# RWKV core: GpSimd inverts 32x32 diagonal blocks, TensorE keeps one doubling level, chain steps are spread anew

## The chip, the cores and the metric

The kernel runs on one core of a Trainium2 chip. The metric is the device time in microseconds of one execution, as the median of several runs. A core has five engines that run side by side and wait for each other by semaphores: TensorE (PE in the profile), VectorE (DVE), ScalarE (ACT), GpSimd (POOL) and SyncE (SP, which here only issues transfers); 16 DMA engines move the data.

## The reference, cut to what matters

The kernel computes one transformer-like block on 512 latent tokens and 256 context tokens, width 2048: a combined input projection, three mixers side by side (gMLP, RWKV-7, neighbourhood attention), an output projection and an MLP. The change touches only the RWKV-7 mixer, 12 heads of width 64, in two directions:

```python
def step(s, inp):
    r_t, w_t, k_t, v_t, a_t, b_t = inp
    sa = jnp.einsum('dbhvk,dbhk->dbhv', s, a_t)
    s = s * w_t[..., None, :] + sa[..., :, None] * b_t[..., None, :] + v_t[..., :, None] * k_t[..., None, :]
    return s, jnp.einsum('dbhvk,dbhk->dbhv', s, r_t)
```

The scan is computed in chunks of 64 tokens. Within a chunk, the term `sa` couples every token to those before it. So each chunk, head and direction needs the inverse of a 64x64 matrix, identity minus a strictly triangular part, and that inverse is what the changed step computes.

## The kernel before, in words

The program is one stream of stages: modulation vectors, the input projection with attention and gMLP, the RWKV projections (to about 1068 us of the profiled execution), the RWKV core (about 1064 to 1560 us), then output projection and MLP, which keep TensorE busy to the end. The core goes over 6 pairs of heads, j = 0 to 5. The two heads of a pair lie on partitions 0 to 63 and 64 to 127. Along the free dimension lie 24 instances of 64 columns: 12 chunks of 64 tokens in 2 directions.

A "block group" is what `blocks` issues: 16 matmuls of 64x64 (8 instances, 2 heads) into one PSUM bank. One such matmul leaves two records in the trace, so a group shows as 32. For one pair the engines do this, and TensorE has it in this order:

- `lows(j+1)`: the strictly triangular matrices of the next pair, 3 groups and 24 matmuls more (line 821). DVE masks them into LT and LG.
- `inverse(j)`: the 64x64 inverses X and their transposes XT. The 16x16 blocks on their diagonals come ready from GpSimd. Two levels (`LEVELS = [16, 32]`) double the block size: 6 groups "inv", 3 groups "invX" (only the first level must also update X itself) and 6 groups "invT". ACT copies each "inv" result to TT, and DVE places the others under a mask (`copy_predicated`, line 1631). The first group waits for the diagonal blocks (`R["xl"]`).
- z and w (6 groups), `read(j-1)` (line 872) and the mean of pair j-1, `front(j+1)` (7 masked products, 11 turns of operands), tr, nk, rc, `values(j+1)`.
- `chain(j-1, n)`, n = 1 to 10: the sequential pass over the chunks. A step is 4 matmuls (8 records, line 860) for the two directions, then two DVE operations (line 1680); the next step waits for those. Steps 1 to 3 stand beside `lows`, steps 4 to 10 between the groups of `inverse`. `read` needs all ten.

GpSimd's part: SP gathers the diagonal blocks of LG and LT into a DRAM image by 16 transfers (`gather`, lines 522 and 523) and loads the image into Y (line 526), where each of 96 partitions holds two 16x16 blocks. GpSimd does forward substitution in place, for k = 1 to 14 one product and one sum (lines 614 and 615), and turns the result into YT (line 616). SP writes Y and YT to DRAM (4 transfers, lines 532 and 533) and reads them into X and XT by 16 transfers (`scatter`, line 539). Between two pairs GpSimd clears X and XT (lines 619 and 621), since the doubling levels write outside the diagonal.

SP issues in the order written in the code: `gather(j)`, `load_vectors(j+1)`, `scatter(j)`, `load_receptances(j+1)`, `load_late(j)`. `load_vectors(j+1)` (lines 494 to 497, 2.7 MB) waits until `front(j)` has used up the old vectors, and `scatter(j)` is issued behind it. The gather of pair j+1 and its inversion run while TensorE works on pair j. The names in the code's loops are those of the pair being gathered, so in the stretch in which TensorE inverts pair j, SP goes through `gather(j+1)`, `load_vectors(j+2)`, `scatter(j+1)`.

A table `USES` gives every product its PSUM bank and the counts to wait for. It is made by `bank_uses`, which lists the products in TensorE's order.

Of the kernel before, what the change touches and what calls it, by code (L numbers as in the profile page):

```python
# [26 lines left out]
P = 128  # L27
# [26 lines left out]
LEVELS = [16, 32]  # L54
BASE = 16
T = 64
# [36 lines left out]
CHAIN_BESIDE_LOWS = {1: 1, 2: 2, 4: 3}  # L93
# [18 lines left out]
def bank_uses():  # L112
# [28 lines left out]
    for j in range(BPAIRS):  # L141
# [80 lines left out]
def build_block(nc, ada, adarows, stream1, stream2, tokens, xtok, small, bias, lnrows, loraw, out):  # L222
    with ExitStack() as es:
# [4 lines left out]
        lowd, ximg, xtimg = (nc.dram_tensor(n, (8 * NC, 2 * BASE * BASE), F32, kind="Internal").ap()  # L228
# [94 lines left out]
        masks = fc(SMALL_B)  # L323
        pick = lambda n: masks[:, P * n:P * n + P]
        eye = masks[:, P * (2 + 2 * len(LEVELS)):]
        LG, product, Y = fc(NC * T), fc(112), fc(512)
        AH, BH, KH = fc(NI * T), fc(NI * T), fc(NI * T)
        BT, KTT, GT, cV, RH = [fc(NI * T)], [fc(NI * T)], fc(NI * T), fc(TOK), [fc(NL * T)]
        fc(13312 - SMALL_B - NC * T - 112 - 512 - 6 * NI * T - TOK - NL * T)
# [6 lines left out]
        LT = [fc(NI * T)]  # L336
# [7 lines left out]
        fc(10 * SEQ)  # L344
        LT.append(fc(NI * T))
        YT = fc(512)
# [8 lines left out]
        late_h, late_l = ([fm(SEQ, F32R) for _ in range(5)] for _ in range(2))  # L355
# [86 lines left out]
        def subbed(j):  # L442
            return 2 + SUB_STEPS * (j + 1) + 2 * max(0, j - 1)
# [13 lines left out]
        def _(sp):  # L457
# [29 lines left out]
            sp.dma_start(masks, small["b"]).then_inc(R["load"], 16)  # L487
# [24 lines left out]
            def packed(a, d):  # L512
                return a[0:8 * NC, BASE * BASE * d:BASE * BASE * (d + 1)]

            def rows_of(q, a):
                return a[BASE * q:BASE * q + BASE].rearrange("r (c s) -> r c s", s=T)[:, :, BASE * (q % 4):BASE * (q % 4) + BASE]

            def gather(j):
                ready(sp, ("lowT", j, 0), ("lowT", j, 1), ("lowT", j, 2), ("low", j, 0), ("low", j, 1))
                for q in range(8):  # L520
                    to = lowd[NC * q:NC * q + NC].rearrange("c (d r s) -> d r c s", d=2, s=BASE)
                    sp.dma_start(to[0], rows_of(q, LG)).then_inc(R["lg"], 16)
                    sp.dma_start(to[1], both_dirs(LT[j % 2])[BASE * q:BASE * q + BASE, :, 1, BASE * (q % 4):BASE * (q % 4) + BASE]
                                 ).then_inc(R["lg"], 16)
                sp.wait_ge(R["lg"], 256 * (j + 1))
                sp.dma_start(Y[0:8 * NC], lowd).then_inc(R["yl"], 16)

            def scatter(j):
                sp.wait_ge(R["sub"], subbed(j))
                sp.wait_ge(R["xl"], 256 * j)  # L530
                for d in range(2):
                    sp.dma_start(packed(ximg, d), packed(YT if d else Y, d)).then_inc(R["img"], 16)
                    sp.dma_start(packed(xtimg, d), packed(Y if d else YT, d)).then_inc(R["img"], 16)
                sp.wait_ge(R["img"], 64 * (j + 1))
                if j:
                    sp.wait_ge(R["sub"], subbed(j) + 2)
                for q in range(8):
                    for to, image in ((X, ximg), (XT, xtimg)):
                        sp.dma_start(rows_of(q, to), image[NC * q:NC * q + NC].rearrange("c (d r s) -> r (c d) s", d=2, s=BASE)
# [5 lines left out]
            gather(0)  # L545
            load_vectors(1)
# [38 lines left out]
        def _(pool):  # L585
# [20 lines left out]
            a = Y[0:96, :].rearrange("p (h r s) -> p h r s", h=2, r=BASE)  # L606
            at = YT[0:96, :].rearrange("p (h r s) -> p h r s", h=2, r=BASE)
            for j in range(BPAIRS):
                pool.wait_ge(R["yl"], 16 * (j + 1))
                step(G.memset(Y[0:96, :].rearrange("p (h e) -> p h e", h=2)[:, :, 0:BASE * BASE:BASE + 1], 1.0))  # L610
# [1480 lines left out]
```

## Time and profile before

| what | us |
|---|---|
| median of 3 runs (range) | 3180.15 (3172.73 to 3182.63) |
| profiled execution | 3187.81 |
| its span, first to last instruction | 3186.0 |
| PE busy | 2948.1 (93%) |
| DVE busy | 1478.7 (46%) |
| POOL busy | 1135.3 (36%) |
| ACT busy | 686.0 (22%) |

The span is what the trace covers; 1.8 us of the profiled execution lie around it. PE is nearly always busy, but its busy time counts slow and overlapping matmuls as well. So what the change is worth must be read in the core, stretch by stretch.

### The profile page before, as it was taken

The numbers are of one execution on the slowest core, as the hardware profiler recorded it, in microseconds if no ns is written. First come the engines' busy times: TensorE is split into PE (matmuls) and PEld (weight loads), VectorE is DVE, ScalarE is ACT, GpSimd is POOL, SyncE is SP. The second block draws the span as 40 slices with busy tenths as digits, with TensorE's granted clock in tenths as the row PEclk, the third lists the DMA queues.
The fourth block names the chain that finished last, engine by engine and source line by source line (L and its number), as shares of the span: only waits on it lengthen the run. The fifth ranks groups of instructions, "written<-read, shape, count | busy, mean of one in ns | idle before, by whom it ended". The sixth has DMA issues, their size and how long they took to land.

```text
span 3186.0 us, 59462 instructions
## 1 busy us (share of the span) xinstructions
PE 2948.1 (93%) x24772; PEld 2420.3 (76%) x24772; DVE 1478.7 (46%) x1845; ACT 686.0 (22%) x1013; POOL 1135.3 (36%) x674
## 2 busy tenths in 40 slices
PE   5799998899998489999998999999999999999996
PEld 0577886687777489988786888888888888888885
DVE  0676677444866534444425433333333343333336
ACT  0222222102222112122113212122221212122221
POOL 0343343434342112210343444444444444444442
PEclk7799998899999799999999999999999999999998
DMA  9675566532433432223432332332332233233322
GB/s 402 237 242 179 193 216 214 178 79 65 156 104 126 150 80 66 67 71 107 185 94 66 93 99 93 94 99 93 94 98 93 93 98 95 93 96 96 94 93 112
DMA packets 164890, 398.57 MB, mean 125 GB/s; under 512 B 73952, under 2 KB 78048, under 8 KB 157856
## 3 DMA queue, kind: packets, MB, share of 16 engines
q1 hardware_dynamic: 134016, 296.00, 28.9%
q10 hardware_dynamic: 30336, 96.64, 8.7%
q8 instruction: 217, 3.56, 0.5%
q0 software_dynamic: 288, 2.10, 0.2%
q14 instruction: 33, 0.27, 0.0%
HBM read 358.89 MB, written 35.80 MB: 124 GB/s over the span
## 4 chain that ended last, share of the span: by engine, by line
PE 62%; DVE 2%; issue 1%; DMA 0%; ACT 0%; POOL 0%; POOLq 0%; SPq 0%; DVEq 0%; ACTq 0%
PE bank L1062 17%; PE bank L1063 16%; PE bank L1061 16%; PE bank L784 7%; PE bank L800 2%; PE bank L872 1%; PE bank L946 1%; PE bank L944 1%; PE bank L860 1%; DVE buf L1928 0%; DVE buf L1929 0%; PE bank L808 0%; DMA buf<-lnrows 0%; DVE buf L1885 0%; DMA buf<-scaled_keys 0%
## 5 line engine op out<-in xcount | busy, mean ns | idle before, releaser
L627 POOL TENSOR_TENSOR buf<-buf 128x1024 fp32r<-128x1024 f32 x288 | 697.7, 2423 | 1015.9 <-ACT buf L1261 1015.9
L1062 PE MATMUL bank<-buf 128*128 128x512 f32 x2304 | 909.0, 395 | 0.0
L1063 PE MATMUL bank<-buf 128*128 128x512 f32 x2304 | 908.1, 394 | 0.0
L1061 PE MATMUL bank<-buf 128*128 128x512 f32 x2304 | 904.5, 393 | 0.5 <-POOL buf L627 0.4
L1261 ACT CAST buf<-buf 128x1024 fp32r<-128x1024 f32 x288 | 303.4, 1053 | 1262.7 <-PE bank L1063 1261.4
L1061 PEld LDWEIGHTS bank<-buf 128*128 128x128 f32 x2304 | 433.1, 188 | 104.7 <-issue 2.8
L1062 PEld LDWEIGHTS bank<-buf 128*128 128x128 f32 x2304 | 432.4, 188 | 101.6 <-issue 0.5
L1063 PEld LDWEIGHTS bank<-buf 128*128 128x128 f32 x2304 | 432.5, 188 | 96.8
L651 PE MATMUL bank<-buf 128*128 128x512 f32 (+1 forms) x1168 | 431.3, 369 | 20.4 <-POOL buf L594 11.8
L652 PE MATMUL bank<-buf 128*128 128x512 f32 (+1 forms) x1168 | 422.9, 362 | 0.0
L653 PE MATMUL bank<-buf 128*128 128x512 f32 (+1 forms) x1168 | 418.1, 358 | 0.0
L1900 DVE TENSOR_TENSOR buf<-buf 128x512 f32<-128x512 f32 x64 | 156.3, 2442 | 440.0 <-ACT buf L1450 439.5
L592 POOL CAST buf<-buf 128x1024 fp32r<-128x1024 f32 x94 | 112.5, 1197 | 640.7 <-PE bank L653 495.1
L784 PE MATMUL bank<-buf 64*64 64x64 f32 x7488 | 260.4, 225 | 45.2 <-issue 37.1
L784 PEld LDWEIGHTS bank<-buf 64*64 64x64 f32 x7488 | 247.3, 141 | 57.0 <-issue 49.1
L1912 DVE TENSOR_TENSOR buf<-bank,buf 128x512 f32<-128x512 f32 x128 | 88.4, 691 | 413.0 <-PE bank L1063 385.0
L651 PEld LDWEIGHTS bank<-buf 128*128 128x128 f32 x1168 | 225.6, 193 | 67.2 <-issue 21.1
L653 PEld LDWEIGHTS bank<-buf 128*128 128x128 f32 x1168 | 224.8, 192 | 34.7
L652 PEld LDWEIGHTS bank<-buf 128*128 128x128 f32 x1168 | 226.2, 194 | 31.5 <-issue 1.2
L594 POOL TENSOR_TENSOR buf<-buf 128x1024 fp32r<-128x1024 f32 x94 | 243.3, 2589 | 7.5
L1751 DVE SCALAR_TENSOR_TENSOR buf<-buf 128x1024 f32<-128x1024 f32 x120 | 194.3, 1656 | 17.8 <-DMA buf<-adarows 17.6
L1914 DVE TENSOR_TENSOR buf<-buf 128x512 f32<-128x512 f32 x128 | 182.0, 1422 | 17.0
(222 smaller groups left out, 2214.8 us busy)
## 6 DMA issues: line engine op xcount, KB each, us to landing
buf<-stream SPq DMA_DIRECT2D x382, 512.0 KB, 3.6
buf<-adarows ACTq DMA_DIRECT2D x108, 512.0 KB, 4.9
buf<-ada SPq DMA_DIRECT2D x32, 1024.0 KB, 13.1
scaled_keys<-buf ACTq DMA_DIRECT2D x18, 768.0 KB, 5.7
buf<-scaled_keys SPq DMA_DIRECT2D x18, 768.0 KB, 6.7
buf<-adarows SPq DMA_DIRECT2D x20, 512.0 KB, 6.9
buf<-tokens SPq DMA_DIRECT2D x4, 1536.0 KB, 21.2
buf<-bias ACTq DMA_DIRECT2D x6, 1024.0 KB, 6.4
```

The lines of the kernel that those rows point to most:

```text
L594: G.tensor_tensor(wl[n % RING1], raw[n % RINGW], wh[n % RING1].bitcast(F32), ALU.subtract).then_inc(split, 1)
L627: G.tensor_tensor(wl2[b % SPLIT2], raw2[b], wh2[b % SPLIT2].bitcast(F32), ALU.subtract).then_inc(split2, 1)
L651: pe.matmul(dst, wh[slot][:, c:c + P], xh[:, k, cols], start=k == 0, stop=False)
L652: pe.matmul(dst, wh[slot][:, c:c + P], xl[:, k, cols], start=False, stop=False)
L653: mm = pe.matmul(dst, wl[slot][:, c:c + P], xh[:, k, cols], start=False, stop=k == KT - 1)
L784: mm = pe.matmul(bank[hs, T * i:T * i + T], lhs[hs, left(c, d) if left else inst(c, d)], rhs[hs, right(c, d) if right else inst(c, d)], st ...
L1061: pe.matmul(bank[:, :], lh, rh, start=start, stop=False)
L1062: pe.matmul(bank[:, :], lh, rl, start=False, stop=False)
L1063: return pe.matmul(bank[:, :], ll, rh, start=False, stop=stop)
L1261: nc.scalar.copy(wh2[pos % SPLIT2], raw2[pos % RING2]).then_inc(high2, 1)
L1751: ins = V.scalar_tensor_tensor(part, rring[i % RINGR], csil[:, k, 0:1], part, ALU.mult, ALU.add)
L1914: t.step(V.tensor_tensor(xr[:, m, cols], xr[:, m, cols], dtmp[m % 2], ALU.add))
```

## The change

The diagonal blocks become 32x32 (`BASE = 32`), one on each of 96 partitions. GpSimd's substitution goes over k = 1 to 30. TensorE keeps the level that joins two 32x32 blocks into 64x64 (`LEVELS = [32]`): 3 groups "inv" and 3 groups "invT", none of "invX". X is then never written outside its diagonal blocks, and its clearing between pairs goes. Gather and scatter-read need 8 transfers each instead of 16, of twice the bytes per row. Chain steps 1 to 5 stand beside `lows`, 6 to 10 in the shorter `inverse`. Buffers Y, YT, LG, product and the identity `eye` move to other addresses; `eye` gets a load of its own behind the stores of the RWKV projections.

```diff
-LEVELS = [16, 32]
-BASE = 16
+LEVELS = [32]
+BASE = 32
-CHAIN_BESIDE_LOWS = {1: 1, 2: 2, 4: 3}
+CHAIN_BESIDE_LOWS = {0: 1, 1: 2, 2: 3, 3: 4, 4: 5}
...
         for x in range(NX + 1):
             if x < NX:
                 add(("inv", j, x), x % 2, "s")
+            if j and x in (1, 2):
+                chain(j - 1, 5 + 2 * x)
             if x:
...
-            if j:
-                chain(j - 1, 4 + x)
+            if j and x < NX:
+                chain(j - 1, 6 + 2 * x)
...
-                for q in range(8):
-                    to = lowd[NC * q:NC * q + NC].rearrange("c (d r s) -> d r c s", d=2, s=BASE)
+                for q in range(4):
+                    to = lowd[NI * q:NI * q + NI].rearrange("(c d) (r s) -> d r c s", d=2, s=BASE)
                     sp.dma_start(to[0], rows_of(q, LG)).then_inc(R["lg"], 16)
...
                 for d in range(2):
-                    sp.dma_start(packed(ximg, d), packed(YT if d else Y, d)).then_inc(R["img"], 16)
-                    sp.dma_start(packed(xtimg, d), packed(Y if d else YT, d)).then_inc(R["img"], 16)
+                    sp.dma_start(direction(ximg, d), direction(YT if d else Y, d)).then_inc(R["img"], 16)
+                    sp.dma_start(direction(xtimg, d), direction(Y if d else YT, d)).then_inc(R["img"], 16)
                 sp.wait_ge(R["img"], 64 * (j + 1))
                 if j:
-                    sp.wait_ge(R["sub"], subbed(j) + 2)
-                for q in range(8):
+                    sp.wait_ge(R["sub"], subbed(j) + 1)
+                for q in range(4):
...
             gather(0)
+            sp.wait_ge(F["hst"], 64 * BPAIRS)
+            sp.wait_ge(F["ost"], 16 * BPAIRS)
+            sp.dma_start(eye, small["b"][:, SMALL_B - T:]).then_inc(setup, 16)
             load_vectors(1)
...
                 for k in range(1, BASE - 1):
-                    rows, shape = BASE - 1 - k, [96, 2, BASE - 1 - k, k]
-                    part = product[0:96, 0:2 * rows * k].rearrange("p (h r s) -> p h r s", h=2, r=rows)
-                    step(G.tensor_tensor(part, a[:, :, k + 1:, k:k + 1].to_broadcast(shape), a[:, :, k:k + 1, 0:k].to_broadcast(shape), ALU.mult))
-                    step(G.tensor_tensor(a[:, :, k + 1:, 0:k], a[:, :, k + 1:, 0:k], part, ALU.add))
-                step(G.tensor_copy(at.rearrange("p h r s -> p h s r"), a))
+                    rows, shape = BASE - 1 - k, [96, BASE - 1 - k, k]
+                    part = product[0:96, 0:rows * k].rearrange("p (r s) -> p r s", r=rows)
+                    step(G.tensor_tensor(part, a[:, k + 1:, k:k + 1].to_broadcast(shape), a[:, k:k + 1, 0:k].to_broadcast(shape), ALU.mult))
+                    step(G.tensor_tensor(a[:, k + 1:, 0:k], a[:, k + 1:, 0:k], part, ALU.add))
+                step(G.tensor_copy(at.rearrange("p r s -> p s r"), a))
                 if j:
                     ready(pool, ("inv", j - 1, NX - 1))
-                    step(G.memset(X, 0.0))
                     ready(pool, ("z", j - 1, 2), ("w", j - 1, 2))
                     step(G.memset(XT, 0.0))
```

The same moves of the chain stand in TensorE's `inverse` and in VectorE's loop.

On TensorE, the first pair with a chain (j = 1), from its third chain step on. Before (L784 is a block group's matmul, x16 one group; L860 a chain step's; L821 the rest of `lows`):

```order
L784 MATMUL bank<-buf 64x64 x16
L860 MATMUL bank<-buf 64x64 x4
L784 MATMUL bank<-buf 64x64 x48
L860 MATMUL bank<-buf 64x64 x4
L784 MATMUL bank<-buf 64x64 x48
L860 MATMUL bank<-buf 64x64 x4
L784 MATMUL bank<-buf 64x64 x48
L860 MATMUL bank<-buf 64x64 x4
L784 MATMUL bank<-buf 64x64 x32
```

Now, the whole stretch from the fourth chain step to the last (L788, L864 and L825 are the same lines as L784, L860 and L821 before):

```order
L825 MATMUL bank<-buf 64x64 x16
L864 MATMUL bank<-buf 64x64 x4
L825 MATMUL bank<-buf 64x64 x8
L864 MATMUL bank<-buf 64x64 x4
L788 MATMUL bank<-buf 64x64 x16
L864 MATMUL bank<-buf 64x64 x4
L788 MATMUL bank<-buf 64x64 x16
L864 MATMUL bank<-buf 64x64 x4
L788 MATMUL bank<-buf 64x64 x16
L864 MATMUL bank<-buf 64x64 x4
```

Between two chain steps there stood up to three groups in the inverse; now there is one, and every part of `lows` has a step behind it.

On SP, the scatter of a pair and the transfers ahead of it. Before (L494 begins the loads of the next pair's vectors, L532 writes the DRAM image, L539 reads it):

```order
L494 DMA buf<-scaled_keys 128x1536
L495 DMA buf<-scaled_keys 128x1536
L496 DMA buf<-scaled_keys 128x1536
L497 DMA buf<-values_bonus_gates 128x768
L532 DMA inverse_blocks<-buf 96x256
L533 DMA turned_inverse_blocks<-buf 96x256
L532 DMA inverse_blocks<-buf 96x256
L533 DMA turned_inverse_blocks<-buf 96x256
L539 DMA buf<-inverse_blocks 16x24x16
```

Now:

```order
L496 DMA buf<-scaled_keys 128x1536
L497 DMA buf<-scaled_keys 128x1536
L498 DMA buf<-scaled_keys 128x1536
L499 DMA buf<-values_bonus_gates 128x768
L534 DMA inverse_blocks<-buf 48x1024
L535 DMA turned_inverse_blocks<-buf 48x1024
L534 DMA inverse_blocks<-buf 48x1024
L535 DMA turned_inverse_blocks<-buf 48x1024
L541 DMA buf<-inverse_blocks 32x24x32
```

The order is the same; the image's rows are 4 KB instead of 1 KB, and the reads are 8 of 32x24x32 instead of 16 of 16x24x16.

## Rows read from the trace of the kernel before

**Rows 1.** Stretches: us; busy PE, PEld, DVE, ACT, POOL; granted clock, DMA share, GB/s

```profile
1119.68:1181.81 62.13, 57.26 (x1848) 56.44 (x1849) 23.34 (x38) 13.19 (x23) 13.44 (x32) 0.97 0.30 76
1181.81:1255.88 74.07, 66.77 (x2101) 64.50 (x2101) 33.28 (x60) 16.28 (x27) 13.42 (x32) 0.98 0.27 71
1255.88:1328.64 72.76, 67.04 (x2101) 64.54 (x2101) 33.34 (x60) 15.00 (x26) 13.40 (x32) 0.97 0.28 73
1328.64:1401.04 72.40, 68.22 (x2101) 65.92 (x2101) 33.34 (x60) 15.00 (x26) 13.41 (x32) 0.96 0.28 72
1401.04:1466.40 65.36, 62.41 (x1957) 60.31 (x1958) 30.02 (x53) 14.99 (x26) 13.40 (x32) 0.97 0.22 46
```

**Rows 2.** Timeline of PE (start, duration): two groups in a row; inverse(3)'s first group

```profile
1290.69 1.10 PE L800 MATMUL bank<-buf 64*64 64x64 f32 x32
1291.62 1.10 PE L784 MATMUL bank<-buf 64*64 64x64 f32 x32
...
1325.47 0.43 PE L860 MATMUL bank<-buf 64*64 64x64 f32 x7
1328.64 1.97 PE L784 MATMUL bank<-buf 64*64 64x64 f32 x32 [2.74 <-issue]
```

**Rows 3.** Timeline of SP's issues: first gather and scatter; scatter(3), then gather(4)

```profile
1075.65 0.32 SPq L522 DMA_DIRECT2D diagonal_blocks<-buf  x1
...
1090.89 0.32 SPq L526 DMA_DIRECT2D buf<-diagonal_blocks  x1
...
1109.53 0.32 SPq L539 DMA_DIRECT2D buf<-inverse_blocks  x1
...
1306.25 0.34 SPq L494 DMA_DIRECT2D buf<-scaled_keys  x1
...
1308.91 0.37 SPq L532 DMA_DIRECT2D inverse_blocks<-buf  x1
...
1317.40 0.32 SPq L539 DMA_DIRECT2D buf<-inverse_blocks  x1
...
1325.74 1.29 SPq L539 DMA_DIRECT2D buf<-turned_inverse_blocks  x1
...
1328.19 0.32 SPq L522 DMA_DIRECT2D diagonal_blocks<-buf  x1
...
1336.00 0.45 SPq L523 DMA_DIRECT2D diagonal_blocks<-buf  x1
```

**Rows 4.** Timeline of POOL: first and last instruction of an inversion; inversion(4) starts

```profile
1093.37 0.15 POOL L610 MEMSET buf<- 96x32 f32 x1 [66.96 <-DMA buf<-diagonal_blocks]
...
1105.21 1.06 POOL L616 COPY buf<-buf 96x512 f32<-96x512 f32 x1
...
1342.22 0.15 POOL L610 MEMSET buf<- 96x32 f32 x1 [51.90 <-DMA buf<-diagonal_blocks]
```

**Rows 5.** Groups on POOL by form, 1090 to 1432 us (busy us, mean ns)

```profile
L616 POOL COPY buf<-buf 96x512 f32<-96x512 f32 x6 | 6.3, 1055 | 0.4
...
L615 POOL TENSOR_TENSOR buf<-buf 96x112 f32<-96x112 f32 x12 | 4.9, 407 | 0.9
...
L614 POOL TENSOR_TENSOR buf<-buf 96x28 f32<-96x28 f32 x12 | 2.8, 237 | 1.1 <-POOL buf L610 0.2
```

**Rows 6.** Timeline of DVE: in front(3), the output of pair 1; two later operations

```profile
1302.89 0.68 DVE L1640 TENSOR_TENSOR buf<-buf 128x512 f32<-128x512 f32 x1
...
1306.11 0.69 DVE L1645 TENSOR_TENSOR buf<-buf 128x512 fp32r<-128x512 f32 x1
...
1554.74 3.35 DVE L1637 RECIPROCAL buf<-buf 128x512 f32<-128x512 f32 x1 [6.38 <-ACT buf L1293]
...
2017.98 1.93 DVE L1914 TENSOR_TENSOR buf<-buf 128x512 f32<-128x512 f32 x1
```

**Rows 7.** Timeline of POOL beside the last two rows of the group above

```profile
1555.82 2.40 POOL L627 TENSOR_TENSOR buf<-buf 128x1024 fp32r<-128x1024 f32 x1 [5.34 <-ACT buf L1261]
...
2016.96 2.40 POOL L627 TENSOR_TENSOR buf<-buf 128x1024 fp32r<-128x1024 f32 x1 [3.15 <-ACT buf L1261]
```

More of the change, by code:

```diff
@@ L322, in build_block @@
         fc = lambda n, dt=F32: take(n, dt, core)
-        masks = fc(SMALL_B)
+        masks = fc(SMALL_B - T)
         pick = lambda n: masks[:, P * n:P * n + P]
-        eye = masks[:, P * (2 + 2 * len(LEVELS)):]
-        LG, product, Y = fc(NC * T), fc(112), fc(512)
+        LT = [None, fc(NI * T)]
         AH, BH, KH = fc(NI * T), fc(NI * T), fc(NI * T)
         BT, KTT, GT, cV, RH = [fc(NI * T)], [fc(NI * T)], fc(NI * T), fc(TOK), [fc(NL * T)]
-        fc(13312 - SMALL_B - NC * T - 112 - 512 - 6 * NI * T - TOK - NL * T)
+        fc(13312 - SMALL_B + T - 7 * NI * T - TOK - NL * T)
         VT, late, RB, RK = [fc(TOK)], [fc(2 * SEQ)], [fc(NL * T)], [fc(NL * T)]
@@ L335, in build_block @@
         AT, GV, TT, XT, X = (fc(NI * T) for _ in range(5))
-        LT = [fc(NI * T)]
+        LT[0] = fc(NI * T)
         VT.append(fc(TOK))
@@ L343, in build_block @@
         TR = fc(NI * T)
-        fc(10 * SEQ)
-        LT.append(fc(NI * T))
-        YT = fc(512)
+        fc(8 * SEQ)
+        Y, YT, LG, product, eye = fc(1024), fc(1024), fc(NC * T), fc(240), fc(T)
         core.close()
@@ L354, in build_block @@
         over_tr = [fm(SEQ, F32R) for _ in range(NI * T // SEQ)]
-        late_h, late_l = ([fm(SEQ, F32R) for _ in range(5)] for _ in range(2))
+        late_h, late_l = ([fm(SEQ, F32R) for _ in range(4)] for _ in range(2))
+        late_h.append(fm(SEQ, F32R))
+        late_l.append(fm(SEQ, F32R))
         mix.close()
@@ L442, in subbed @@
         def subbed(j):
-            return 2 + SUB_STEPS * (j + 1) + 2 * max(0, j - 1)
+            return 2 + SUB_STEPS * (j + 1) + max(0, j - 1)
         block = es.enter_context(nc.Block())
@@ L486, in _ @@
             sp.wait_ge(used1, N1)
-            sp.dma_start(masks, small["b"]).then_inc(R["load"], 16)
+            sp.dma_start(masks, small["b"][:, 0:SMALL_B - T]).then_inc(R["load"], 16)
             def load_vectors(j):
@@ L892, in inverse @@
                         if x == 0:
-                            pe.wait_ge(R["xl"], 256 * (j + 1))
+                            pe.wait_ge(R["xl"], 128 * (j + 1))
                         blocks(("inv", j, x), LT[j % 2], X, g)
+                    if j and x in (1, 2):
+                        chain(j - 1, 5 + 2 * x)
                     if x:
@@ L902, in inverse @@
                         blocks(("invT", j, y), TT, XT, gy)
-                    if j:
-                        chain(j - 1, 4 + x)
+                    if j and x < NX:
+                        chain(j - 1, 6 + 2 * x)
             pe.wait_ge(z_ev, TILES[-1][-1][2])
@@ L1663, in lows @@
                 if n == 0:
-                    dve.wait_ge(R["lg"], 256 * j)
+                    dve.wait_ge(R["lg"], 128 * j)
                 if n < 3:
@@ L1700, in dve_core @@
                 for x in range(NX + 1):
+                    if j and x in (1, 2):
+                        chain(j - 1, 5 + 2 * x)
                     if x:
@@ L1706, in dve_core @@
                         placed(("invT", j, y), XT, 3 + 2 * l, g)
-                    if j:
-                        chain(j - 1, 4 + x)
+                    if j and x < NX:
+                        chain(j - 1, 6 + 2 * x)
                 for g in range(3):
@@ L1718, in dve_core @@
                     key = ("tr", j, g)
+                    if j == 0 and g == 0:
+                        dve.wait_ge(setup, 80)
                     V.tensor_tensor(wide8(TR, g), eight(use(dve, key)), eye[:, None, :].to_broadcast([P, 8, T]), ALU.add
```

22 lines of the change are left out of this document (11 added, 11 removed).

## The prediction

> **What bounds the kernel now.** I read the stretches of the core first, one from the first group of inverse(j) to that of inverse(j+1) [rows 1]; I call these starts I0 to I5, so I0 is 1119.68 and I5 is 1466.40. Three full stretches take 74.07, 72.76 and 72.40 us, and in them PE is busy for 67 to 68 us. DVE (33 us) and POOL (13.4 us) have room. So PE is near the bound, but not alone: in front of I3 it idles 2.74 us [rows 2]. The view calls this "issue", yet SP's timeline names the releaser: the last read of the diagonal blocks is issued at 1325.74 and takes 1.29 us [rows 3], and PE starts at 1328.64, when it has landed. The idle time costs again afterwards: the first group behind it takes 1.97 us where a group at full clock takes 1.10 us [rows 2], since the clock had fallen in the idle time to the lower of its two levels (1.2 instead of 2.4 GHz; group times 1.97 and 1.10).
>
> Then I followed the loop of GpSimd backwards from I3 [rows 3]. The scatter's first write is issued at 1308.91, right behind load_vectors (1306.25), which waited for front(3). POOL had begun inversion 3 long before. An inversion lasts from 1093.37 to 1105.21 + 1.06 = 1106.27, 12.9 us [rows 4]. The one for pair 4 starts at 1342.22, 13.6 us behind I3, and would be over at I3 + 26.5, while the scatter in the stretch before went out 53.0 us behind its I2 = 1255.88. So a ready result waits some 26 us for its turn on SP. This is the cover in which a longer inversion may hide.
>
> **The change, part by part.**
>
> *TensorE, removed.* A pair loses 3 groups inv, 3 invX and 3 invT, 9 of 32 records. Two groups in a row start 1291.62 - 1290.69 = 0.93 us apart [rows 2], so 9 x 0.93 = 8.4 us a pair, 50 us over six. That is the most that can be won, apart from idle time that goes too.
>
> *GpSimd, added.* Before, 28 operations work on 2,240 elements per partition. Now 60 operations work on 2 x (30 x 1 + 29 x 2 + ... + 1 x 30) = 9,920. From 237 ns at 28 elements (a product) and 407 ns at 112 (a sum) [rows 5] the slope is 2.0 ns an element at most; with 10 ns of it put down to the sum, 1.9, and 0.19 us are left at zero elements. The whole before, 12.9 us, less the copy (1.06) and the clearing of the diagonal (about 0.25), is 11.6 us for 28 operations, which leaves 0.07 to 0.08 us between two. So: 60 x (0.19 + 0.08) = 16.2, 9,920 x 1.93 ns = 19.1, copy 2 x 1.06 = 2.1, clearing 0.25: 37.7 us. From below, 36.5 (slope 1.8). From above, the nearest long operation is 2.40 us for 1,024 elements [rows 7], 2.16 ns each, which makes 40. I take 37.8.
>
> *GpSimd and DVE together.* The inversion now reaches into the time in which DVE makes the output of the pair before: four products or sums of two SBUF operands, 0.69 us each, between 1302.89 and 1306.80 [rows 6]. Such an operation excludes one of POOL's: at 2017.98 one took 1.93 us and ended 0.55 us behind POOL's operation, which began at 2016.96 and took 2.40 [rows 6, 7]; 0.69 is its plain length. The reciprocal (3.35 us) excludes nothing: POOL's 2.40 us went by beside it at 1555.82. So POOL loses about 4 x 0.69 plus the cast, 3.2 us, in the stretches 1 to 4; between 0 and 7 (if the reciprocal counts). DVE loses at most one short operation of POOL's each time, some 2 us, within its idle 40 us.
>
> The Trainium skill, "SBUF — State Buffer", section "SBUF: two separate sides", says that the port pair shared by VectorE and GpSimd is an exclusive lock, held for a whole instruction. By that rule, the trace agrees in the product and not for the reciprocal; held to the letter for the reciprocal too, it would make the loss 6.5 us in each of four stretches and the sum 13 us worse; without any lock the sum would be 13 us better.
>
> *Transfers.* The gather loses 8 of its 16 issues. 16 take from 1328.19 to 1336.45, 0.5 us each [rows 3], so POOL starts 13.6 - 3.9 = 9.7 us behind I. The total of packets is the same, of 128 B instead of 64 B; if packets and not issues set the pace, nothing is saved (13.6). The scatter's writes take 3.3 us when nothing is ahead of them (1106.27 to 1109.53) and 8.5 behind load_vectors (1308.91 to 1317.40) [rows 3, 4]. The reads take 1328.64 - 1317.40 = 11.2 us for 16, so 11.2 - 8 x 0.5 = 7.3 for 8; 11.2 at worst, 6 at best.
>
> *Not costed.* The memset of X (1.4 us) goes from behind the inversion, where it hid. The load of `eye` waits for stores issued at about 1075 and stands ahead of load_vectors(1), which waits until 1095 anyway. Chain steps 1 to 5 beside `lows` wait for each other somewhat more (a step with its DVE half took 0.8 us where nothing stood between), but they run ahead of I, where PE idles for the diagonal blocks; steps 6 to 10 may cost 1 us. The moved buffers cost nothing.
>
> *The sum.* New loop of GpSimd: 9.7 + 37.8 + 3.2 + 3.3 + 7.3 = 61.3 us. The loads go out at about I + 42 (front is 8.4 us earlier than 50.4) and are nearly over when the writes start at I + 50.7. TensorE's own loop: 72.76 - 2.74 - 8.4 = 61.6, and 74.07 less the same is 62.9. The two are level: I take 62.
>
> - I0: POOL starts some 5 us earlier (8 issues less in front of 1090.89), then 37.8 - 12.9 = 24.9 longer, then reads 3 shorter: +17 us. PE has nothing to do here, so all of this is paid.
> - I0 to I1: 9.7 + 37.8 + 3.3 + 7.3 = 58.1 against 62.1: -4.0.
> - I1 to I2, I2 to I3, I3 to I4: 62 against 74.1, 72.8, 72.4: -12.1, -10.8, -10.4.
> - I4 to I5: 61.4 against 65.4, in which PE did not wait: -4.0.
> - Behind I5: -8.4, +2.5 for the lower clock after a wait that wasn't there, +1 for the chain: -5.
>
> Together -29 us. Everything behind the core is PE-bound and only moves forward. The profiled execution, 3187.8, would become 3159; it lies 7.7 us above the median of the runs, so the median becomes 3180.15 - 29 = 3151 us.
>
> **The rivals.**
>
> 1. *GpSimd stays in the cover.* The inversion is 36.5 us, nothing excludes, reads take 6. Then its loop is 56 us and PE sets the pace at about 59.5, since without idling it keeps its clock. I0 +14, then -6, three times -13 and I4 to I5 -7, tail -7: -45 us, 3135. For it speaks that the inversion before took the same 12.9 us beside a busy and beside an idle DVE; against it, that it needs every term at its favourable end.
>
> 2. *The gain is eaten.* Transfers of the same number of packets save nothing (gather 13.6, reads 11.2), or exclusion costs 7 us. The first adds 7.8 us to each of five loops and to I0, and PE's loop, level with GpSimd's, hides none of it: -29 + 6 x 7.8 = +18 at its full size, at half of it -6, so 3174 us, which I take for it. The even pace of 0.5 us per issue at 192 as at 384 packets speaks against the full size; the occasional issue of 1.2 us and more [rows 3] speaks for some.
>
> 3. *Slower: the long inversion.* If an element costs over 2.6 ns, since rows are now 32 elements apart and the patterns are longer, the inversion is above 44 us. The loop is then 68 us and I0 +24; each further us counts six times. It breaks even at 37.8 + 29 / 6 = 42.6 us and is slower by 0.3% from about 44.2 us. At 46 us it is 20 us slower, 3200. For it speaks only the 2.16 ns of the long operation, against it that the operation at k = 1 (28 rows of one element) and at k = 14 (2 rows of 14) cost the same 230 to 250 ns.
>
> The Trainium skill, "GPSIMD Engine Reference", section "Performance pitfalls for Q7 kernels", gives about 2.9 instead of 1.9 cycles for an element read at a stride above 8 bytes. As an estimate from that page, 9,920 elements would then take 24 us, the inversion 43 us, and the change would end near zero. The product already reads one column at a stride of 64 B in this trace, at 1.9 ns an element, so this rule adds nothing that the rows don't hold; it is part of rival 3.
>
> **How the numbers follow.** The forecast has 0.58, with a range of its own from -42 to -13 us (3138 to 3167): each us of inversion counts six times. Rival 1 has 0.17, rival 2 0.15, rival 3 0.06; 0.04 are for a start of the core that is delayed otherwise. A difference below 0.3%, 9.5 us, is about what a measurement of this kernel can't tell from none. Faster: forecast and rival 1 and a third of rival 2 with a little less, 0.82; same 0.11; slower 0.07. The range leaves out the lowest and the highest tenth: 3131 to 3180.
>
> **What would show it.** POOL's inversion: 60 operations in 35 to 36 us, 37.8 with the copy; 41 in the stretches 1 to 4, where a single operation of POOL's takes 0.7 us longer. I0 at about 1137; the stretches at 58, 62, 62, 62, 61. PE's records fall by 1,728. PE idles for the reads in front of every I, and its first groups behind run at the lower clock. SP issues the scatter behind POOL's copy, not behind load_vectors. Wrong would be: stretches above 66, an inversion above 42 us, or stretches below 60 in which PE never waits (rival 1).

## The result, and the profile after

| | kernel before | changed kernel |
|---|---|---|
| median (lowest to highest) | 3181.39 us (3172.73 to 3185.61) | 3147.80 us (3139.02 to 3149.67) |
| profiled execution | 3187.81 | 3147.17 |
| its span | 3186.0 | 3145.1 |

The ratio is 0.9895 (95% interval 0.9876 to 0.9915): 33 us faster, where 29 were forecast. A later comparison (experiment 11) gave 0.9886 (0.9871 to 0.9902).

I take the profiled executions apart at these marks: the first block group of the core (C), I0, I5, the start of the last reciprocal on VectorE (R) and the end. "Core" is C to R.

| | to C | C to I0 | I0 to I5 | I5 to R | core | R to end |
|---|---|---|---|---|---|---|
| before | 1064.3 | 55.4 | 346.7 | 88.4 | 490.4 | 1631.3 |
| changed | 1056.6 | 73.3 | 308.9 | 79.8 | 462.0 | 1626.6 |
| difference | -7.8 | +17.9 | -37.8 | -8.6 | -28.5 | -4.7 |

The part ahead of C has the same code in both; in the other profiles of this study C lies anywhere from 1051.6 to 1062.6, so the 7.8 us are no effect of the change. The core gives 28.5 us, and 4.7 come from a place that the forecast had left at zero, the hardware loop of the MLP.

The stretches of the changed kernel, to be held against [rows 1] (columns as there):

```profile
1129.83:1188.52 58.69, 48.94 (x1576) 48.28 (x1577) 19.75 (x36) 11.41 (x20) 33.45 (x63) 0.94 0.39 103
1188.52:1251.56 63.04, 60.25 (x1812) 57.71 (x1814) 29.85 (x52) 14.49 (x24) 34.83 (x63) 0.95 0.39 107
1251.56:1314.73 63.17, 57.40 (x1817) 54.84 (x1815) 30.90 (x57) 13.21 (x23) 34.82 (x63) 1.00 0.35 91
1314.73:1377.19 62.46, 57.63 (x1812) 54.95 (x1813) 29.98 (x53) 13.22 (x23) 34.84 (x63) 1.00 0.39 109
1377.19:1438.74 61.55, 54.02 (x1669) 51.11 (x1669) 28.12 (x51) 13.21 (x23) 34.92 (x63) 0.98 0.24 54
```

58.7, 63.0, 63.2, 62.5 and 61.6 us, forecast 58.1, 62, 62, 62 and 61.4. PE has some 288 records fewer in a stretch (1,728 in all, as forecast), POOL is busy for 33 to 35 instead of 13.4 us.

PE's timeline in front of I0, I1, I2, I3 and I5, to be held against [rows 2]:

```profile
1129.83 3.38 PE L788 MATMUL bank<-buf 64*64 64x64 f32 x60 [28.64 <-issue]
...
1188.52 1.98 PE L788 MATMUL bank<-buf 64*64 64x64 f32 x32 [8.22 <-issue]
...
1251.23 0.52 PE L864 MATMUL bank<-buf 64*64 64x64 f32 x8 [0.37 <-DVE buf L1686]
1251.56 1.14 PE L788 MATMUL bank<-buf 64*64 64x64 f32 x32
...
1314.73 1.15 PE L788 MATMUL bank<-buf 64*64 64x64 f32 x32 [1.42 <-issue]
...
1438.74 1.97 PE L788 MATMUL bank<-buf 64*64 64x64 f32 x32 [4.32 <-issue]
```

PE waits 28.6, 8.2, 0, 1.4 and 4.3 us for the diagonal blocks. In I0, I1 and I5 GpSimd's loop decides, at I2 (and I4, whose group has no idle time either) TensorE, at I3 both arrive nearly together. The first group takes 1.15 us behind a wait of 1.4 us, at a granted clock of 1.00, and 1.97 behind one of 4.3, at 0.50: in this profile only the longer idle times brought the clock down to 1.2 GHz.

SP's timeline of scatter(2), to be held against [rows 3] (L496 load_vectors, L534 the first write, L541 the first and the last read):

```profile
1229.60 0.34 SPq L496 DMA_DIRECT2D buf<-scaled_keys  x1
...
1237.11 0.49 SPq L534 DMA_DIRECT2D inverse_blocks<-buf  x1
...
1242.12 0.32 SPq L541 DMA_DIRECT2D buf<-inverse_blocks  x1
...
1246.31 1.50 SPq L541 DMA_DIRECT2D buf<-turned_inverse_blocks  x1
```

The loads go out 7.5 us ahead of the first write, which now waits for POOL alone. POOL's timeline: the start of inversion(0), its sum of 198 elements and its last instruction, then of inversion(3) the start, three operations beside VectorE's output, and the end, to be held against [rows 4]:

```profile
1081.22 0.15 POOL L615 MEMSET buf<- 96x32 f32 x1 [62.00 <-DMA buf<-diagonal_blocks]
...
1107.77 0.57 POOL L620 TENSOR_TENSOR buf<-buf 96x198 f32<-96x198 f32 x1
...
1115.96 1.91 POOL L621 COPY buf<-buf 96x1024 f32<-96x1024 f32 x1
...
1263.80 0.15 POOL L615 MEMSET buf<- 96x32 f32 x1 [25.27 <-DMA buf<-diagonal_blocks]
...
1289.10 0.92 POOL L620 TENSOR_TENSOR buf<-buf 96x210 f32<-96x210 f32 x1
1290.10 0.60 POOL L619 TENSOR_TENSOR buf<-buf 96x198 f32<-96x198 f32 x1
1290.77 0.91 POOL L620 TENSOR_TENSOR buf<-buf 96x198 f32<-96x198 f32 x1
...
1300.06 1.94 POOL L621 COPY buf<-buf 96x1024 f32<-96x1024 f32 x1
```

The same time on DVE's timeline, to be held against [rows 6]:

```profile
1284.16 3.34 DVE L1643 RECIPROCAL buf<-buf 128x512 f32<-128x512 f32 x1
...
1288.74 0.83 DVE L1646 TENSOR_TENSOR buf<-buf 128x512 f32<-128x512 f32 x1
...
1290.34 0.90 DVE L1648 TENSOR_TENSOR buf<-buf 128x512 f32<-128x512 f32 x1
1291.27 0.95 DVE L1649 TENSOR_TENSOR buf<-buf 128x512 f32<-128x512 f32 x1
```

Inversion(0), beside which VectorE runs only operations that read one operand from PSUM, lasts from 1081.22 to 1117.87, 36.65 us; the one for pair 3 from 1263.80 to 1302.00, 38.2 us. The difference, 1.5 us, lies where VectorE makes its output. A sum of 0.6 us takes 0.9 there, and VectorE's operation 0.83 to 0.95 instead of 0.68 to 0.69 [rows 6].

The rows say by how much. POOL's sum starts at 1290.77, when VectorE's operation (1290.34, 0.90 us) has 0.47 us to go, and takes 0.34 us more than in inversion(0). VectorE's next one starts at 1291.27, when that sum has 0.41 us to go, and takes 0.26 more. VectorE's one at 1290.34 found POOL's product (1290.10, 0.60 us) with 0.36 to go and took 0.21 more. So each operation is longer by what is left of the other's, less 0.13 to 0.15 us. The pair in [rows 6, 7] fits too: at 2017.98 POOL's operation had 1.38 us to go, and VectorE's took 1.24 more than its 0.69. The rows fit two engines that take turns, an instruction each. Neither lost the other's whole length, since each time the other was under way already.

POOL's groups by form, 1070 to 1500 us, to be held against [rows 5]:

```profile
L621 POOL COPY buf<-buf 96x1024 f32<-96x1024 f32 x6 | 11.7, 1950 | 0.4
...
L620 POOL TENSOR_TENSOR buf<-buf 96x240 f32<-96x240 f32 x12 | 8.0, 670 | 0.9
```

A sum of 240 elements takes 670 ns; the 0.19 us and 1.93 ns an element of the prediction make 0.65.

### The profile page after: what moved, and what is told of

Read it like the earlier page. It is cut to its first block, busy times and chain, and to the rows that moved or that the text cites. A ratio compares the mean times of both kernels' runs of the same rounds, so it can differ in the third digit from the quotient of the medians.

```text
span 3145.1 us, 56010 instructions
## 1 busy us (share of the span) xinstructions
PE 2894.3 (92%) x23044; PEld 2368.9 (75%) x23044; DVE 1453.2 (46%) x1809; ACT 674.2 (21%) x995; POOL 1269.2 (40%) x861
## 4 chain that ended last, share of the span: by engine, by line
PE 61%; issue 2%; DVE 2%; DMA 0%; ACT 0%; POOL 0%; SPq 0%; DVEq 0%; ACTq 0%; POOLq 0%
PE bank L1068 17%; PE bank L1069 17%; PE bank L1067 17%; PE bank L788 6%; PE bank L804 2%; PE bank L876 1%; PE bank L864 1%; PE bank L952 1%; PE bank L950 1%; DVE buf L1938 0%; DVE buf L1939 0%; PE bank L812 0%; DMA buf<-scaled_keys 0%; DVE buf L1895 0%; PE bank L825 0%
## 5 line engine op out<-in xcount | busy, mean ns | idle before, releaser
L1922 DVE TENSOR_TENSOR buf<-bank,buf 128x512 f32<-128x512 f32 x128 | 88.4, 691 | 413.1 <-PE bank L1069 385.1
L788 PE MATMUL bank<-buf 64*64 64x64 f32 x5760 | 203.6, 224 | 59.6 <-issue 52.7
L788 PEld LDWEIGHTS bank<-buf 64*64 64x64 f32 x5760 | 191.2, 140 | 71.2 <-issue 61.5
L1761 DVE SCALAR_TENSOR_TENSOR buf<-buf 128x1024 f32<-128x1024 f32 x120 | 187.2, 1597 | 20.4 <-DMA buf<-adarows 20.1
```

The costliest lines, as they stand in the source:

```text
L788: mm = pe.matmul(bank[hs, T * i:T * i + T], lhs[hs, left(c, d) if left else inst(c, d)], rhs[hs, right(c, d) if right else inst(c, d)], st ...
L1761: ins = V.scalar_tensor_tensor(part, rring[i % RINGR], csil[:, k, 0:1], part, ALU.mult, ALU.add)
```

## The experiments

**1. Is a result of GpSimd's really lying ready for 26 us in the kernel before?** The kernel before, with the inversion made longer by harmless work:

```diff
+                for _ in range(50):
+                    step(G.tensor_tensor(product[0:96, 0:112], Y[0:96, 0:112], Y[0:96, 0:112], ALU.mult))
```

> The kernel before with GpSimd's inversion lengthened alone, by 50 operations of 96x112 behind the substitution (0.48 us apart, so 24 us, to about 37 us). Nothing on TensorE changes. Theory (the scatter's place behind load_vectors on SP covers a longer inversion): I0 +24; I0 to I1 +4 (the inversion ends 10 us after the old turn, but the writes then have no loads ahead of them); the full stretches and I4 to I5 +0 to +1. Together +28 us, 3209 us. Rival (every added us is paid in each of six inversions): +144 us. Rival (the cover is smaller than 26 us, since the loads collide): +40 to +60 us.

Measured: 3205.78 us, ratio 1.0057 (1.0036 to 1.0077), some 18 us slower, less than the 28 expected; in the profiled execution, the longest of the four (3213.61), the core is 29.5 us longer (519.9), of which 20.8 lie ahead of I0. The inversion grew by 22.3 us (12.9 to 35.2). Without cover it would have cost six times that. SP's timeline of a scatter in this kernel (L495 begins the loads, L533 is the first write), POOL's copy having ended at 1326.71:

```profile
1327.71 0.34 SPq L495 DMA_DIRECT2D buf<-scaled_keys  x1
...
1331.24 0.36 SPq L533 DMA_DIRECT2D inverse_blocks<-buf  x1
```

The result is ready 1.0 us before the loads of the vectors go out and 4.5 us before its own write: the cover is there, and it is now nearly used up. I0, which has none, pays nearly in full.

**2. What bounds the changed kernel once GpSimd is fast?** The changed kernel with k up to 14 only; it leaves out a part of the inverse.

```diff
-SUB_STEPS = 2 + 2 * (BASE - 2)
+SUB_STEPS = 2 + 2 * 14
-                for k in range(1, BASE - 1):
+                for k in range(1, 15):
```

> The changed kernel with the substitution stopped at k = 14 of 30, which leaves out 32 operations and 5,440 of 9,920 elements (the inverse is then incomplete): the inversion takes about 19 us less. Theory (GpSimd's loop and TensorE's are level, TensorE has no slack behind it): I0 -19; I0 to I1 -10; the four later stretches -1 to -6 each as the waits and the lower clock behind them go. Together -35 to -42 us against the changed kernel, about 3108 us. Rival (GpSimd's loop alone sets the pace, TensorE is far from its bound): near -100 us. Rival (TensorE alone sets it): -19 us, the first inversion only.

Measured: 3125.85 us, ratio 0.9809 (0.9783 to 0.9835), 27 us less than the changed kernel's ratio gives, for 35 to 42 expected. The inversion is 18.2 us, half of it, and yet the full stretches stay:

```profile
1163.30:1228.96 65.66, 60.08 (x1819) 57.62 (x1817) 29.62 (x55) 14.48 (x24) 17.33 (x31) 0.95 0.36 98
1228.96:1291.58 62.62, 57.46 (x1816) 54.88 (x1814) 29.74 (x57) 13.20 (x23) 17.29 (x31) 1.00 0.36 97
1291.58:1357.01 65.43, 58.88 (x1813) 56.19 (x1813) 28.98 (x54) 13.20 (x23) 17.27 (x31) 0.97 0.37 103
```

In the profile the core is 19.7 us shorter (442.3): 18.4 less from C to I0 and 8 less in the stretches I0 to I1 and I4 to I5, but 5 more in the three full stretches and 1.7 more behind I5. So TensorE's own loop is 62.6 to 65.7 us here, and not the 59.5 of rival 1. In it stand pauses for which the trace has no releaser, in the middle of a row of matmuls whose data are long there:

```profile
1274.52 0.28 PE L950 MATMUL bank<-buf 64*64 64x64 f32 x4
1278.12 0.27 PE L952 MATMUL bank<-buf 64*64 64x64 f32 x3 [3.32 <-issue]
```

Less such pauses of over 0.7 us (4.5, 3.3 and 5.3 us in the three) the stretches are 61.2, 59.3 and 60.1 us, near rival 1's 59.5. The row of the queue that brings instructions, for 1275.0 to 1276.8 us of this kernel (packets, MB, share):

```profile
q8 instruction: 1, 0.02, 3.4%
```

This packet, a fetch of 16.4 KB, landed at 1276.80, 1.3 us before PE went on. It is no single case. In the 14 kept profiles, from I0 to R, there are 162 such pauses, the waits in front of I0 to I5 left out. 146 of them end 1.15 to 1.65 us behind the landing of a fetch, where only 10% of all moments lie so. Experiment 7 shows the same in a loop. Their sum differs between executions: 16.2 us from I0 to R in the changed kernel's first profile and 20.7 in its second (experiment 11).

**3. The price of one more us of inversion.** The changed kernel with ten operations of 112 elements more, 4.4 to 4.6 us:

> The changed kernel with 10 more operations of 96x112 in every inversion, 4.8 us. Theory (the loops are level): I0 and I1 +4.8 each, the stretches from I1 to I4 +3 to +4.5 each since 0 to 2 us of slack are left, I5 +4.8; together +25 us. Rival (TensorE alone sets the pace of the full stretches): +5 to +14 us.

Measured: 3167.37 us, ratio 0.9942 (0.9920 to 0.9964), 15 us slower than the changed kernel, between the 25 of the theory and the rival's 5 to 14; the core is 482.8 us, 20.9 longer: +4.4 ahead of I0, then +3.2, +2.7, +2.9, +4.5, +4.5, and -1.3 behind I5. In the first two full stretches TensorE hides a third and more of it, since the two loops are level, and I0 to I1 hides some too; the other three pay in full. "Each us of inversion counts six times" was too much, it is 4.6 by the profile and 3.3 by the medians.

**4. Issues or packets?** The changed kernel, each of the 8 + 8 transfers cut in two halves of 16 partitions. That makes as many transfers as before with the changed kernel's packets of 128 B; what comes on top of them are packets of 4 B, 16 for each added transfer:

```diff
-                    sp.dma_start(to[0], rows_of(q, LG)).then_inc(R["lg"], 16)
+                    for h in range(2):
+                        sp.dma_start(to[0][16 * h:16 * h + 16], rows_of(q, LG, h)).then_inc(R["lg"], 16)
```

> The changed kernel with each gather and scatter read split into two of 16 rows: 16 and 16 transfers again, with the changed kernel's packets and bytes. Theory (the number of issues sets the length, 0.5 us each): I0 +8, I0 to I1 +8, the others +6 to +8; together +42 us. Rival (packets set the length, as in my second rival): within 5 us of the changed kernel.

Measured: 3192.04 us, ratio 1.0021 (1.0009 to 1.0034), 40 us slower than the changed kernel and no faster than the kernel before. The core is 507.0 us, 45 longer. The stretch from I2, and PE's first groups at I3 and I5, in this kernel:

```profile
1275.36:1347.31 71.95, 59.02 (x1812) 56.71 (x1813) 30.43 (x54) 13.22 (x23) 34.99 (x63) 0.93 0.39 92
```

```profile
1347.31 1.97 PE L790 MATMUL bank<-buf 64*64 64x64 f32 x32 [9.53 <-issue]
...
1484.13 1.97 PE L790 MATMUL bank<-buf 64*64 64x64 f32 x32 [12.50 <-issue]
```

SP's issue of a half takes 0.44 to 0.47 us, that of a whole 0.47 to 0.53, apart from some long ones in both. So the number of transfers sets the pace, and halving it is worth as much as the whole gain. Without it the change would have been worth nothing.

**5. The bare inversion.** Ahead of I0 TensorE and VectorE both idle. VectorE does the first pair's inversion here, with the same 60 operations and the copy:

```diff
+            dve.wait_ge(R["yl"], 16)
...
+                own(V.tensor_tensor(part, a[:, k + 1:, k:k + 1].to_broadcast(shape), a[:, k:k + 1, 0:k].to_broadcast(shape), ALU.mult))
+                own(V.tensor_tensor(a[:, k + 1:, 0:k], a[:, k + 1:, 0:k], part, ALU.add))
+            own(V.tensor_copy(at.rearrange("p r s -> p s r"), a))
...
-            for j in range(BPAIRS):
+            for j in range(1, BPAIRS):
                 pool.wait_ge(R["yl"], 16 * (j + 1))
```

> The changed kernel, but VectorE inverts the diagonal blocks of the first pair with the same 60 operations and the copy, while GpSimd waits for pair 1. In that stretch VectorE has nothing else to do for 28 us of TensorE's idle time. From the trace of the changed kernel: GpSimd's operation of 240 elements takes 0.61 to 0.67 us; VectorE at about 1 ns an element and 0.2 us per operation with its own wait would take 60 x 0.2 + 9.9 + 1 = 23 us instead of 36.7. Theory (the first inversion lies bare on the path, nothing hides it): I0 moves forward by 13 us and the time falls by 11 to 14 us against the changed kernel, ratio to the kernel before 0.9855 instead of 0.9895. Rival: VectorE's masks of pair 1 and its part of front(0) come late, which gives back half: 5 to 7 us. Rival: VectorE's wait behind each own operation costs as much as GpSimd's, no gain.

Measured: 3138.56 us, ratio 0.9852 (0.9834 to 0.9870). DVE's timeline (first, a middle and the last operation) and PE's behind it:

```profile
1088.34 0.09 DVE L1709 MEMSET buf<- 96x32 f32 x1
...
1098.91 0.40 DVE L1714 TENSOR_TENSOR buf<-buf 96x240 f32<-96x240 f32 x1
...
1110.19 1.03 DVE L1715 COPY buf<-buf 96x1024 f32<-96x1024 f32 x1
```

```profile
1112.09 1.12 PE L826 MATMUL bank<-buf 64*64 64x64 f32 x16 [6.86 <-DVE buf L1635]
1123.58 6.63 PE L789 MATMUL bank<-buf 64*64 64x64 f32 x162 [10.36 <-issue]
```

22.9 us instead of 36.65. PE now waits twice, first 6.9 us for VectorE's late masks and then 10.4 us for the blocks, together 17.2 us where it waited 28.6: C to I0 falls from 73.3 to 62.2 us, the core to 449.8. Against the changed kernel's ratio this is 14 us, the upper end of what was expected.

**6 and 7. Where do the 4.7 us behind the core come from?** The rows of the queue with instructions, in 1280 us of the MLP loop, of the kernel before (packets, MB, share):

```profile
q8 instruction: 64, 1.05, 0.3%
```

and of the changed kernel:

```profile
q8 instruction: 1, 0.02, 0.0%
```

The loop's code is the same; what differs is its place behind a shorter core. So I moved it, by semaphore increments that nobody waits for, put in front of inverse(0) where PE idles: 192 in the changed kernel, 64 in the kernel before.

```diff
+                if j == 0:
+                    for _ in range(192):
+                        pe.sem_inc(tick, 1)
                 inverse(j)
```

> The changed kernel with 192 semaphore increments more on TensorE's instruction stream, placed in front of inverse(0), where TensorE idles 28 us. They do nothing but move all later instructions of TensorE by 192 places. The trace of the kernel before shows 64 fetches of instructions in the eight turns of the MLP loop, that of the changed kernel 1, and the part behind the core is 4.6 us shorter. Theory: the fetches depend on where the loop body lies in the instruction stream; a fetch moves 16.4 KB, 256 instructions of 64 B, and the change took away 1728, which is 7 x 256 less 64. With 192 more the loop lies as it did before: the 64 fetches are back and the part from the last reciprocal to the end takes 1631 us instead of 1626.5, the time rises by 4 to 5 us against the changed kernel, and if the increments aren't fully hidden by up to 2 us more. Rival: the 4.6 us have another cause (addresses of buffers, the state at the core's end), and the tail stays at 1626.5.

> The kernel before with 64 semaphore increments on TensorE's stream in front of inverse(0), where TensorE idles. Theory of the loop's place: the loop now lies as in the changed kernel, the fetches fall from 64 to 1 and the part from the last reciprocal to the end from 1631 to 1626.5 us; the time falls by 4 to 5 us, ratio 0.9985. Rival: nothing moves, ratio 1.000 and 64 fetches.

Measured, 192 in the changed kernel: 3152.64 us, ratio 0.9906 (0.9889 to 0.9922), which can't be told from the changed kernel's; the fetches are back (64 in the loop) and R to the end takes 1630.2 us instead of 1626.6. 64 in the kernel before: 3203.21 us, ratio 1.0056 (1.0038 to 1.0073), slower by 18 us, against both expectations; the loop has 64 fetches as before, and R to the end takes 1657.2 us. The queue's row, 1883 to 3186 us, since this loop is longer:

```profile
q8 instruction: 64, 1.05, 0.4%
```

Its PE has a pause at one place in each turn of the loop:

```profile
1912.90 0.79 PE L1066 MATMUL bank<-buf 128*128 128x512 f32 x1 [2.52 <-issue]
...
2095.72 0.51 PE L1066 MATMUL bank<-buf 128*128 128x512 f32 x1 [1.98 <-issue]
...
2277.18 0.52 PE L1066 MATMUL bank<-buf 128*128 128x512 f32 x1 [1.97 <-issue]
```

The pauses end 1.3 to 1.6 us behind the landing of a fetch. They add up to 16 us, and behind five of them the granted clock was 0.50, for 24 us in all, which costs another 12: together most of the 31 us over the changed kernel's 1626.6. The place matters, and by more than I had thought; my count of the instructions was wrong.

**8. The chain's spread, undone in the changed kernel as nearly as its shorter inverse allows.** One of the edits:

```diff
-CHAIN_BESIDE_LOWS = {0: 1, 1: 2, 2: 3, 3: 4, 4: 5}
+CHAIN_BESIDE_LOWS = {1: 1, 2: 2, 4: 3}
```

> The changed kernel, but the chain steps are spread as nearly as possible as before: 1 to 3 beside lows, 4 to 10 in the inverse, which now has only six groups (4 behind inv 0, then one in front of and one behind each invT). It prices the new spread by itself. Prediction's view (the spread is about free: steps 1 to 5 stand ahead of I, 6 to 10 cost about 1 us): within 3 us of the changed kernel either way. Rival: seven steps between six groups, with about 0.8 us for a step with its VectorE half and 0.93 us for a group, make TensorE wait for VectorE up to 1 us at step 10 and at those behind the copies, 2 us a pair: +10 us against the changed kernel. Rival: moving steps away from the stretch ahead of I makes I earlier where GpSimd doesn't bound, and the time falls by up to 5 us.

Measured: 3152.32 us, ratio 0.9902 (0.9882 to 0.9922), not to be told from the changed kernel. By the profile the core is 466.3 us, 4.4 longer, 2.9 of it behind I5.

**9. The new spread alone, in the kernel before.** Steps 1 to 5 beside `lows`, 6 to 10 at their old places in the inverse.

```diff
-CHAIN_BESIDE_LOWS = {1: 1, 2: 2, 4: 3}
+CHAIN_BESIDE_LOWS = {0: 1, 1: 2, 2: 3, 3: 4, 4: 5}
...
-            if j:
+            if j and x > 1:
                 chain(j - 1, 4 + x)
```

> The kernel before with the new spread of the chain alone: steps 1 to 5 beside the five parts of lows, 6 to 10 in the inverse as before (none behind its first two places). GpSimd, the block size and the transfers are untouched. Theory: in the stretches 2 to 4 TensorE idled 2.7 us in front of I for the reads, and the scatter hangs on front(j), so two steps more ahead of I fill that idle time and take 0.8 us each from behind it: 1 to 2 us in each of five stretches, 5 to 8 us in all, ratio 0.998. Then part of the gain of the change was the spread's and not GpSimd's. Rival (the prediction's view, spread about free): within 3 us, ratio 0.999 to 1.001. Rival: steps 1 to 5 wait for VectorE one after the other and push I out: slower by 5 us.

Measured: 3171.47 us, ratio 0.9983 (0.9970 to 0.9995), 5 us faster (2 to 10). The core is 482.6 us, 7.8 shorter. The stretches ahead of I1, I2, I3, I4 and I5 changed by +1.7, -3.9, -0.4, +0.1 and -2.8 us. PE in front of I4:

```profile
1381.77 0.52 PE L860 MATMUL bank<-buf 64*64 64x64 f32 x8 [0.38 <-DVE buf L1680]
1384.18 2.02 PE L784 MATMUL bank<-buf 64*64 64x64 f32 x62 [1.88 <-issue]
```

The fifth step stands in front of the wait now, and the wait is still there. The four waits in front of I1 to I4 add up to 6.9 us, and to 7.4 in the kernel before. So the gain is real, but it is not the filling of these waits, as the theory had it. Much of it isn't the chain's either: 1.6 of the 7.8 us lie ahead of I0, where both kernels have the same code, and 3.7 are pauses of the kind of experiment 2 (17.4 us from I0 to R, for 21.1), no more than they differ by in two executions of one kernel. R to the end, the same code again, takes 1628.2 us with the same 64 fetches, 3.1 less. What the spread is worth by itself isn't settled.

**10. The loop's place, with the right count.**

The queue's row in the same 1280 us of the loop:

```profile
q8 instruction: 1, 0.02, 0.0%
```

The fetches are gone and R to the end takes 1626.6 us, as in the changed kernel: the place of the loop decides whether it fetches. The kernel as a whole is not faster: 3188.09 us, ratio 1.0026 (1.0011 to 1.0041). The increments aren't free. PE was ready 19.24 us ahead of I0 (idle before that group), the last read had landed at 1116.92 and I0 came only at 1125.89: 19.24 / 128 = 0.15 us each, more than the idle time ahead of I0 holds, so I0 is 7.9 us later from C. In experiment 6 the same sum gives 28.96 / 192 = 0.15, and I0 came 2.5 us behind the landing. The theory's ratio of 0.9985 to 0.999 left that out.

**11 and 12. The better version against the changed kernel, on one chip.**

> The changed kernel itself, beside the next run on the same chip. Ratio to the kernel before 0.9895 as measured first (0.988 to 0.991).

> The changed kernel with the first pair's inversion on VectorE, again, beside the changed kernel on the same chip: 12 us faster than that (its core was 12.2 us shorter in the profile, 11.1 of them in front of I0), so a ratio of 0.9852 to the kernel before. Rival: the two differ by less than 5 us, and the first comparison was drift between chips.

Measured: the changed kernel 3143.30 us (0.9886), with the first inversion on VectorE 3134.63 us, ratio 0.9859 (0.9839 to 0.9879). It is 9 us better here and 14 in the first comparison, for 12 expected; the intervals overlap, but both pairs and both profiles (cores of 449.8 and 448.9 us against 462.0 and 463.6) say the same. It is the fastest of the complete kernels tried.

## Why the prediction was right

The kernel time came out at 3147.8 us for a forecast of 3151, the core at -28.5 us for a sum of -29. That the core is so close is partly luck: the five stretches are 3.4 us longer than forecast and the part behind I5 is 3.6 us shorter. Step by step:

- **Cover.** Right: experiment 1 used it up and paid nearly in full only ahead of I0.
- **Inversion, 37.7 us.** 36.65 measured. The slope and the fixed part from [rows 5] carried to four times the elements; the copy was 1.9 us for 2.1.
- **Exclusion, 3.2 us.** 1.5 measured. The step took a whole operation of VectorE's as lost for GpSimd each time. The trace shows that GpSimd waits only for what is left of it, 0.3 us, and that VectorE waits in its turn. The Trainium skill, "SBUF — State Buffer", section "SBUF: two separate sides", has the port pair as a lock held for a whole instruction, which VectorE takes for operations in a 2-port mode or with two SBUF inputs. The trace agrees: the waits above are the rest of the other's instruction less 0.13 to 0.15 us. The prediction held the rule against the reciprocal's row, but a reciprocal has one input, and GpSimd's operations ran on during one of 3.3 us unchanged.
- **Gather, 9.7 us behind I.** 8.3 to 12.2 measured. The issues cost 0.5 us each as read, but between the last one and POOL's start lie up to 7.2 us (1256.63 to 1263.80; in the other gathers 4.6 to 6.0) where I had kept the 5.8 of before (1336.45 to 1342.22 [rows 3, 4]). With the writes at 5 us instead of 3.3 the parts of stretch 2 to 3 are 12.2 + 38.2 + 5.0 + 7.8 = 63.2 us, for 61.3 forecast: the longer start and writes (+4.2) outweighed the shorter inversion (-2.8).
- **Halved transfers.** Right, and the strongest term: experiment 4 took away the halving alone and the whole gain went. The worry that packets set the pace (rival 2) is refuted.
- **TensorE level with GpSimd at 62.** Right: 62.5 to 63.2 us, with waits of 0 to 1.4 us. Rival 1 fell by experiment 2: even with GpSimd fast TensorE took 62.6 to 65.7, of which the pauses are 3.3 to 5.3.
- **Chain spread, 0 to +1 us.** No such cost was measured: alone the spread comes with 5 us less in the kernel before (experiment 9), much of it in places that the chain doesn't touch, and in the changed kernel it is too small to measure (experiment 8). Whether a part of the shorter stretches belongs to it isn't shown.
- **I0, +17.** +17.9. **Behind I5, -5.** -8.6 measured. The lower clock came as allowed for: the first 6.9 us behind I5 had a granted clock of 0.65, which costs some 2.4 us. But the pauses without a releaser are 2.0 us less than before there (4.7 for 6.7; 6.1 in the changed kernel's second profile), which is luck, and the chain's 1 us didn't show.
- **"Everything behind the core only moves forward."** Wrong by 4.7 us, shown by experiments 6 and 10. In four profiles with 64 fetches R to the end takes 1628.2 to 1631.3 us, in the nine with one 1626.1 to 1626.9, so the step is worth 1.3 to 5.2. It is the larger part of what separates -33 from -29.
- **Rival 3** never came near: 2 ns an element also for rows 32 apart.

What stays open: why TensorE pauses inside the core. The pauses end at the same distance behind a fetch as those in the loop of experiment 7, so late instructions are their likely cause, but no run removed them to show it. The increments of experiments 6, 7 and 10 moved the core's code as well, and the sum stayed at 18.8, 21.6 and 19.4 us. In experiment 2 they are 3.3 to 5.3 us of each full stretch.

## What to carry to other kernels

When work is moved from a busy engine to a slower idle one, add up the whole loop of the slower engine, transfers included: here the count of small DMA issues decided as much as the arithmetic, and the loop came out level with the engine it relieved. Look for the one pass of the loop that has no cover, usually the first; it pays in full, and another engine may be idle just there. And before giving a moved or shortened program credit for what happens far behind it, look at the instruction fetches of the later loops, and at pauses amid ready matmuls.

## What the runs showed that I had not expected

- VectorE does the same small fp32 operations in 0.40 us for 240 elements where GpSimd takes 0.61 to 0.70, in 0.20 for 30 elements where GpSimd takes 0.24 to 0.26, and in 22.9 instead of 36.65 us in all: 1.6 times as fast, not more, since the advantage is small on short operations.
